# Meta tokens and inputs loaded in one transfer, the first unit of weights split tile by tile, squares behind the splits

## What is computed

```python
h = jnp.concatenate([meta, x], axis=1)
h = h + 0.5 * _swiglu(_rms_norm(h, norm_ffn1[l]), ffn1_w_gate[l], ffn1_w_up[l], ffn1_w_down[l])
def _rms_norm(x, g):
    y = xf * lax.rsqrt(jnp.mean(xf * xf, axis=-1, keepdims=True) + EPS)
    return (y * g.astype(jnp.float32)).astype(x.dtype)
def _swiglu(x, w_gate, w_up, w_down):
    return (jax.nn.silu(x @ w_gate) * (x @ w_up)) @ w_down
```

## Time and profile before

| | us |
|---|---|
| median of 3 runs | 2344.92 |
| lowest, highest | 2344.82, 2347.24 |
| profiled execution, its own time | 2350.06 |
| its span in the profile | 2348.3 |
| TensorE busy in the span | 2316.8 (99%) |
| VectorE, ScalarE, GpSimd busy | 1504.5, 1041.7, 194.3 |

### The profile page before, as it was taken

The page is one execution under the profiler, slowest core; times in us unless marked ns, Lnnn a source line. Parts: engine busy times, 40 slices in busy tenths (PEclk is TensorE's granted clock), DMA queues, the critical chain, the costliest instruction groups (busy, mean ns, idle before and its releaser), DMA issues.

```text
span 2348.3 us, 47351 instructions
## 1 busy us (share of the span) xinstructions
PE 2316.8 (99%) x17980; PEld 2211.4 (94%) x17980; DVE 1504.5 (64%) x2073; ACT 1041.7 (44%) x1277; POOL 194.3 (8%) x264
## 2 busy tenths in 40 slices
PE   8999999999999999999999999999999999999997
PEld 8999999999999999999999999998888888888886
DVE  6555544467554578888777666557666655666655
ACT  5343433445543343435555544445444433444443
POOL 0000010289200020002000000000000000000000
PEclk9999999999999999999999999999999999999998
DMA  7555555555555545555555545665665655656653
GB/s 214 175 173 175 172 178 175 174 172 171 182 172 174 167 137 170 162 168 160 155 160 159 163 136 180 197 186 174 195 185 182 193 185 185 188 179 196 186 187 119
DMA packets 416922, 408.66 MB, mean 174 GB/s; under 512 B 19408, under 2 KB 416720, under 8 KB 416848
## 3 DMA queue, kind: packets, MB, share of 16 engines
q1 hardware_dynamic: 411856, 407.03, 56.3%
q10 hardware_dynamic: 4992, 0.60, 0.2%
HBM read 405.48 MB, written 2.10 MB: 174 GB/s over the span
## 4 chain that ended last, share of the span: by engine, by line
PE 96%; DVE 2%; ACT 1%; issue 0%; DMA 0%; ACTq 0%; DVEq 0%; SPq 0%
PE ps L358 31%; PE ps L356 21%; PE ps L357 21%; PE ps L353 20%; PE ps L530 0%; PE ps L474 0%; DVE w_lo L902 0%; DVE xs L1058 0%; DMA raw<-gate 0%; ACT w_hi L599 0%; PE ps L523 0%; DVE scr L925 0%; ACT xs L621 0%; PE ps L537 0%; ACT scr L608 0%
## 5 line engine op out<-in xcount | busy, mean ns | idle before, releaser
L902 DVE TENSOR_TENSOR w_lo<-raw,w_hi 128x1024 fp32r<-128x1024 f32 x765 | 949.0, 1246 | 631.4 <-ACT w_hi L599 624.2
L358 PE MATMUL ps<-xs,w_lo 128*128 128x256 f32 (+2 forms) x4416 | 1260.0, 285 | 0.0
L599 ACT ACTIVATE w_hi<-raw 128x1024 fp32r<-128x1024 f32 x765 | 805.0, 1058 | 940.5 <-PE ps L358 931.6
L356 PE MATMUL ps<-xs,w_hi 128*128 128x272 f32 (+2 forms) x3008 | 866.7, 288 | 10.1 <-DVE xs L1058 3.5
L357 PE MATMUL ps<-xs,w_hi 128*128 128x272 f32 (+2 forms) x3008 | 863.9, 287 | 0.0
L358 PEld LDWEIGHTS ps<-xs,w_lo 128*128 128x128 f32 x4416 | 836.6, 189 | 0.0
L356 PEld LDWEIGHTS ps<-xs,w_hi 128*128 128x128 f32 x3008 | 570.3, 190 | 15.6 <-issue 10.1
L357 PEld LDWEIGHTS ps<-xs,w_hi 128*128 128x128 f32 x3008 | 572.8, 190 | 0.0
L353 PE MATMUL ps<-xs,w_hi 128*128 128x512 f32 x1408 | 493.3, 395 | 0.3 <-DVE w_lo L902 0.3
L358 PE MATMUL ps<-hs,w_lo 128*128 (+2 forms) x1408 | 402.6, 286 | 0.0
L353 PEld LDWEIGHTS ps<-xs,w_hi 128*128 128x128 f32 x1408 | 264.5, 188 | 61.2 <-issue 0.6
(11 more groups left out here) (249 smaller groups left out, 1602.0 us busy)
## 6 DMA issues: line engine op xcount, KB each, us to landing
raw<-gate SPq DMA_DIRECT2D x176, 512.0 KB, 4.5
raw<-up SPq DMA_DIRECT2D x176, 512.0 KB, 3.8
raw<-down SPq DMA_DIRECT2D x176, 512.0 KB, 4.3
raw<-w_in SPq DMA_DIRECT2D x168, 512.0 KB, 3.5
raw<-w_out SPq DMA_DIRECT2D x32, 512.0 KB, 4.2
raw<-w_proj SPq DMA_DIRECT2D x24, 512.0 KB, 4.7
raw<-glu_a SPq DMA_DIRECT2D x8, 512.0 KB, 3.4
raw<-glu_b SPq DMA_DIRECT2D x8, 512.0 KB, 3.4
```

The costliest lines, as they stand in the source:

```text
L356: pe.matmul(out, hi, xh, start=start and k == 0, stop=False)
L358: last = pe.matmul(out, lo, xh, start=False, stop=stop and k == KT - 1)
L599: act.activation(w_hi[:, slot, :, :], raw[:, slot, :, :], ACT.Copy).then_inc(hi_ready, 1)
L902: tt(w_lo[:, slot, :, :], raw[:, slot, :, :], w_hi[:, slot, :, :].bitcast(f32), SUB).then_inc(lo_ready, 1)
```

## The change

- **One transfer for `h`.** The host puts meta tokens and inputs into one array `hT` (rows of 272 floats). `metaT` and its wait are gone.
- **Unit 0 tile by tile.** SyncE loads tile 0 of `h`, tile 0 of the weights, tile 1 of both, then tiles 2 and 3 of both, then whole units. ScalarE and VectorE scale and split unit 0 tile by tile, and TensorE waits per tile (`first_lo`); in units 0 to 3 it goes by tiles of `x` (`by_tile`).
- **Splits first.** For units 1 to 3 the split of the weights comes ahead of the scalings. The squares come behind the split of unit 4; the splits of units 5 and of 6 to 8 are put among and behind them. Squares 0 to 2 are computed by GpSimd.
- **Norm later.** `norm(0)` is issued behind unit 5 instead of unit 3.
- **Small transfers** go from ScalarE to SyncE, between the loads of units 8 to 11, and the small operations on `lb` to the end of the first half of the network.
- **Start.** GpSimd sets `ones` first; `keep_warm` needs only that and makes 9 products instead of 14.

```diff
-                sp.wait_ge(lo_ready, u + 1)
+                if not isinstance(u, int) or u >= RING:
+                    sp.wait_ge(lo_ready, u + 1)
...
-            def load_x(c):
-                sp.dma_start(h[:, 4 * c:4 * c + 4, META:T],
-                             xT.rearrange("(k p) t -> p k t", p=P)[:, 4 * c:4 * c + 4, :]).then_inc(x_in[c], 16)
-                if c == 0:
-                    sp.dma_start(h[:, :, 0:META], metaT.rearrange("(k p) t -> p k t", p=P)).then_inc(meta_in, 16)
+            def load_x(k0, k1, landed):
+                sp.dma_start(h[:, k0:k1, :], hT.rearrange("(k p) t -> p k t", p=P)[:, k0:k1, :]).then_inc(landed, 16)
+            def load_first(w):
+                for c, (k0, k1) in enumerate(((0, 1), (1, 2), (2, 4))):
+                    load_x(k0, k1, x_first[c] if c < 2 else x_in[0])
+                    sp.dma_start(raw[:, 0, k0:k1, :], w.rearrange("(k p) n -> p k n", p=P)[:, k0:k1, 0:NC])\
+                        .then_inc(w_first[c] if c < 2 else raw_ready[0], 16)
+                for j in range(1, 4):
+                    load_x(4 * j, 4 * j + 4, x_in[j])
+                    load(j, w, j, 0, j)
+            def load_small(j):
+                if j == 0:
+                    sp.dma_start(sv[:, 0:3, :], s5v).then_inc(small_in[1], 16)
+                    sp.dma_start(lb[:, :, :], hg_lb).then_inc(small_in[2], 16)
+                elif j == 1:
+                    sp.dma_start(hgn[:, :], hg_norm).then_inc(small_in[3], 16)
+                    sp.dma_start(dsk[:, :], s5d).then_inc(small_in[4], 16)
+                elif j == 2:
+                    sp.dma_start(btmp[:, 0:2 * ST * GP].rearrange("p (r j c) -> p r j c", r=2, j=ST), s5b)\
+                        .then_inc(small_in[5], 16)
+                else:
+                    sp.wait_ge(consts, 2)
+                    for g in range(2):
+                        sp.dma_start(cd[64 * g:64 * g + 64, :, :, g * GP:(g + 1) * GP], s5c[64 * g:64 * g + 64])\
+                            .then_inc(small_in[6 + g], 16)
             def ffn(w_gate, w_up, w_down, q):
                 first = 0
                 for blocks in HALVES:
...
                     if peeled:
-                        column_block(w_gate, 0, 0, load_x)
+                        load_first(w_gate)
                         column_block(w_up, 0, 1)
-                    with sp.Fori(peeled, blocks) as b:
+                        column_block(w_gate, NC, 2, load_small)
+                        column_block(w_up, NC, 3)
+                    with sp.Fori(2 * peeled, blocks) as b:
                         column_block(w_gate, (b + first) * NC, b * 2 + q)
                         column_block(w_up, (b + first) * NC, b * 2 + q + 1)
                     q += 2 * blocks
@@ -339,13 +370,18 @@
...
+                first = isinstance(u, int) and u < RING
+                if not first:
+                    pe.wait_ge(lo_ready, u + RING + 1)
                 by_column = [(c, k) for c in range(2) for k in range(KT)]
                 by_row = [(c, k) for k in range(KT) for c in range(2)]
                 for c, k in by_column if need is None else by_row:
                     if need is not None and c == 0:
                         pe.wait_ge(x_ready, need + k + 1)
+                    if first and c == 0 and j == 0 and k < KT - 1:
+                        pe.wait_ge(first_lo, k + 1)
+                    elif first and c == 0 and k == (0 if j else KT - 1):
+                        pe.wait_ge(lo_ready, u + RING + 1)
...
                 for _ in range(n):
-                    pe.matmul(ps[:, bank, 0:P], ones[:, :], ident[:, :], start=True, stop=True)
+                    pe.matmul(ps[:, bank, 0:P], ones[:, :], ones[:, :], start=True, stop=True)
...
             def column_block(q, banks, c0, x_need, between=None, fresh=False, wide=False):
                 for j in range(4):
-                    if j or not fresh:
+                    by_tile = fresh and (j == 0 or isinstance(q, int) and q == 0)
+                    if not by_tile:
                         pe.wait_ge(x_ready, x_need + 4 * j + 4)
                     unit(j, 4 * q + j, banks, T - c0, rows(xs, 4 * j, c0, T - c0), j == 0, j == 3,
-                         None if j or not fresh else x_need, wide)
+                         x_need + 4 * j if by_tile else None, wide)
...
                         column_block(b * 2 + q, 0, c0, f * 2 * DT, fresh=mean, wide=f == 1)
-                        if mean:
+                        if mean and f:
                             norm(2 * f, c0)
                         pe.wait_ge(hidden, b + done + 1)
-                        column_block(b * 2 + q + 1, 2, c0, f * 2 * DT, wide=f == 1)
+                        column_block(b * 2 + q + 1, 2, c0, f * 2 * DT,
+                                     lambda j: norm(0, c0) if mean and not f and j == 1 else None, wide=f == 1)
...
-            pe.wait_ge(consts, 2)
-            keep_warm(14, 0)
+            pe.wait_ge(ones_ready, 1)
+            keep_warm(9, 0)
+            pe.wait_ge(consts, 1)
...
                     def block(b, mean=False):
-                        for j in range(1 if mean and not f else 0, 4):
+                        start = mean and not f
+                        for j in range(3 if start else 0, 4):
                             split(b * 2 + q, j)
+                        if start:
+                            split(b * 2 + q + 1, 0)
+                            split(b * 2 + q + 1, 1)
                         if mean:
                             root(2 * f, c0)
-                        split(b * 2 + q + 1, 0)
+                        if not start:
+                            split(b * 2 + q + 1, 0)
...
-                        for j in range(1, 4):
+                        for j in range(2 if start else 1, 4):
...
             act.wait_ge(small_in[0], 16)
-            for c in range(4):
+            for k in range(KT):
+                act.wait_ge(x_first[k] if k < 2 else x_in[0], 16)
+                upper(0, 0, k)
+                act.wait_ge(w_first[k] if k < 2 else raw_ready[0], 16)
+                act.activation(w_hi[:, 0, k, :], raw[:, 0, k, :], ACT.Copy).then_inc(first_hi if k < KT - 1 else hi_ready, 1)
+            for c in range(1, 4):
+                act.wait_ge(raw_ready[c], 16)
+                act.activation(w_hi[:, c, :, :], raw[:, c, :, :], ACT.Copy).then_inc(hi_ready, 1)
                 act.wait_ge(x_in[c], 16)
                 for k in range(4 * c, 4 * c + 4):
                     upper(0, 0, k)
-                if c < LEAD:
-                    act.wait_ge(raw_ready[c], 16)
-                    act.activation(w_hi[:, c, :, :], raw[:, c, :, :], ACT.Copy).then_inc(hi_ready, 1)
-                else:
-                    split(0, 0)
-                if c < 2:
-                    square(0, 0, 2 * c)
-                    square(0, 0, 2 * c + 1)
-            act.dma_start(sv[:, 0:3, :], s5v).then_inc(small_in[1], 16)
-            act.dma_start(lb[:, :, :], hg_lb).then_inc(small_in[2], 16)
-            act.dma_start(hgn[:, :], hg_norm).then_inc(small_in[3], 16)
-            act.dma_start(dsk[:, :], s5d).then_inc(small_in[4], 16)
-            act.dma_start(btmp[:, 0:2 * ST * GP].rearrange("p (r j c) -> p r j c", r=2, j=ST), s5b).then_inc(small_in[5], 16)
-            for k in range(4, DT // 2):
+            split(0, 1)
+            act.wait_ge(sq_ready, 3)
+            for k in range(3, DT // 2):
                 square(0, 0, k)
-            for g in range(2):
-                act.dma_start(cd[64 * g:64 * g + 64, :, :, g * GP:(g + 1) * GP], s5c[64 * g:64 * g + 64])\
-                    .then_inc(small_in[6 + g], 16)
+                if k == 4:
+                    split(0, 2)
...
                         else:
                             tt(gate, ps[:, 0:2, 0:T], inverse, MUL).then_inc(gated, 1)
-                        split(b * 2 + q + 1, 0)
+                        if not start:
+                            split(b * 2 + q + 1, 0)
                         dve.wait_ge(sig_ready, b + done + 1)
                         tt(gate, gate, sig, MUL).then_inc(silu, 1)
-                        split(b * 2 + q + 1, 1)
+                        if not start:
+                            split(b * 2 + q + 1, 1)
                         dve.wait_ge(silu, b * 2 + 2 * done + 1)
                         tt(gate, gate, inverse, MUL).then_inc(silu, 1)
...
+                    if between and not first:
+                        between(0)
...
+                if stage == 0:
+                    dve.wait_ge(small_in[2], 16)
+                    step(tt(lbt[:, 2, :], lb[:, 0, :], lb[:, 1, :], ALU.max))
+                    step.join()
+                    step(tt(lbt[:, 0, :], lb[:, 0, :], lbt[:, 2, :], SUB))
+                    step(tt(lbt[:, 1, :], lb[:, 1, :], lbt[:, 2, :], SUB))
...
             dve.wait_ge(small_in[0], 16)
-            for c in range(4):
+            for k in range(KT):
+                lower(0, 0, k)
```

(37 more changed lines are left out.)

22 lines of the change are left out of this document (9 added, 13 removed).

## The result

| | before | after |
|---|---|---|
| median of 20 runs | 2345.43 us | 2342.19 us |
| lowest and highest | 2343.23, 2347.65 | 2340.69, 2343.89 |
| profiled execution | 2350.06 | 2342.97 |
| its span, its mean granted clock | 2348.3, 0.993 | 2341.3, 0.995 |

The ratio is 0.9987, with a 95% interval of 0.9981 to 0.9993. The kernel is 3.2 us (0.13%) faster, where 7.2 were forecast: a real gain, but inside the 0.2% that the prediction called no change, and 0.8 us above the upper end of its range. The two profiled executions are 7.1 us apart, as summed.

The account below looks back on a forecast made before the run. TensorE's own matmuls (96% of the span) were taken as the bound. Terms up to the ninth unit, 1.45+1.2+2.87+2.8-0.8-0.3 = 7.2 us, gave 2344.9-7.2 = 2337.7 us, range 2334.8 to 2341.4.

Parts of the forecast that it names:

- gap ahead of unit 2: Start of the kernel: squares no longer stand between units 2 and 3, so the wait goes, 1.2 us won.
- wait ahead of unit 4: Cd transfers leave ScalarE's queue and the norm moves behind unit 5, so TensorE's wait goes: 2.87 us won.
- unit 5 waits for the squares' chain: Squares and additions now stand among the splits, so unit 5 is ready late: 0.8 us lost.
- unit 6 starts: ScalarE's split of unit 6 stands behind the last square: 0.3 us lost, start at 31.5.
- load of unit 11: Queued behind the cd pair, issued at some 39.3, landing near 43; 1.4 us of cover remain, costs nothing.
- rival C: GpSimd's third square meets unit 1's lower split, which starts 1.2 us later: 2338.9, chance 0.08.
- the term of 2.8 us for the half clock: TensorE's clock is at half from 30 to 36 us in before; with the gap gone, 2.8 us won.
- loads' term: Without the meta transfer, loads land 1.4 us earlier; unit 1 starts at 13.25 instead of 14.70, 1.45 us won.
- A: Clock falls after TensorE's 2.05 us idle behind unit 0, costing 1.7 us net: 2339.4, chance 0.25.
- B: Start of the kernel: nothing lands earlier from memory, unit 1 at 14.65, first term gone: 2339.1, chance 0.10.
- D: Weights land 1 us or more earlier still, VectorE's 2.97 per unit paces: 2336.7 to 2336.3, chance 0.12.
- E: Slower than before: the low clock holds on from unit 1, above 2345, chance 0.02.

Follow-up runs that it names:

- b_again: The kernel before, unchanged, measured once more: 2346.16 us, ratio 1.0002.
- a_again: The kernel after, unchanged, measured once more: 2342.27 us, ratio 0.9986.
- b_filled: Before, with 11 more products that nobody reads filling TensorE's wait ahead of unit 4: 2345.10 us, ratio 1.0.
- b_cd_moved: Before, with only the two cd transfers moved from ScalarE's queue to SyncE's, ahead of unit 11's load: 2342.88 us, ratio 0.9989.
- b_one_load_cd: Before, with one transfer for meta tokens and inputs and the cd pair moved to SyncE: 2340.74 us, ratio 0.9981.
- b_one_load: Before, with only the one transfer for meta tokens and inputs: 2342.90 us, ratio 0.9991.
- a_unit0_whole: After, with unit 0's input and weights in one transfer each, split, scaled and multiplied as a whole: 2341.74 us, ratio 0.9985.
- a_pad: After, with the rows of hT padded in memory from 1088 to 1280 bytes: 2342.24 us, ratio 0.9988.
- a_filled: After, with 16 warm-up products for 9 and 5 more between units 0 and 1: 2342.16 us, ratio 0.9988.
- a_all_filled: After, with fills at the start, in two waits of the projection behind the second norm and ahead of the last head: 2340.59 us, ratio 0.9982.
- b_two_filled: Before, with the one transfer, the cd pair on SyncE, and fills behind the second norm and ahead of the last head: 2339.81 us, ratio 0.9976.
- a_whole_filled: After, with unit 0 whole, 25 warm-up products instead of 9, and the three later waits filled: 2340.13 us, ratio 0.9981.

## Why the prediction was wrong

**The mechanism was right.** Held against the profile, the steps stand:

| step | forecast | in after's profile |
|---|---|---|
| unit 1's weights land, unit 1 starts | 10.4, 13.25 | 11.2, 13.98 |
| gap ahead of unit 2 | gone | gone (it starts at 17.1, was 18.94) |
| wait ahead of unit 4 | gone | gone (23.1, was 29.91 behind the norm) |
| unit 5 waits for the squares' chain | 0.8 | 0.51 |
| unit 6 starts | 31.5 | 32.00 |
| unit 8 starts | 37.55 | 38.10 |
| the span | 2341 | 2341.3 |

That the last row agrees is in part luck. After's profile has the clock low for 6.8 us at the last head, as before's has; with the 0 of b_again and a_again there, the two spans are 2343.0 and 2339.4.

The load of unit 11 is covered as said. SyncE's timeline in after:

```profile
32.31 3.29 SPq L314 DMA_DIRECT2D cd<-s5c  x2
35.64 2.51 SPq L269 DMA_DIRECT2D raw<-gate  x1
```

It is issued at 35.64, was forecast at 39.3, and landed at 41.4; TensorE waited nowhere there. GpSimd's squares and VectorE's lock are there too, in GpSimd's and VectorE's timeline:

```profile
6.00 2.34 POOL L1396 TENSOR_TENSOR scr<-h 128x544 f32<-128x544 f32 x2 [2.39 <-DMA h<-hT]
...
6.43 0.95 DVE L952 SCALAR_TENSOR_TENSOR xs<-h,gain,xs 128x272 fp32r<-128x272 f32 x1 [1.57 <-ACT xs L660]
7.31 1.31 DVE L1086 TENSOR_TENSOR w_lo<-raw,w_hi 128x256 fp32r<-128x256 f32 x1
```

A lower half took 0.95 us for the 0.50 of the first one, a quarter's split 1.31 for the first one's 0.42. It cost nothing, since unit 1's weights were not there yet; rival C did not come. The Trainium skill (SBUF — State Buffer, Who interferes with whom) gives VectorE and GpSimd one shared, exclusively locked port pair; the trace agrees, as it did at the earlier trace rows.

**The step that failed is the term of 2.8 us for the half clock**, with the sentence that carried it over to the median: "the saving is in absolute microseconds, so 2344.9-7.2". The 7.2 were the distance to one execution of before, and that execution was not like the median. It held 6.8 us of low clock in each of three places (30, 828, 1364) besides some 11 at its end, and took 5.1 us more than the median shown. The prediction had that 5.1 in its hands, and added the 2.8 of the first low stretch to the saving all the same. b_filled shows what that term is worth in the median: 0, with 2.1 as the end of its interval. Two more pairs agree: b_cd_moved gains 2.3 where 2.3 to 2.9 us of wait went, and b_one_load_cd is 2.2 ahead of b_one_load where 2.5 went. None of them rules out a microsecond. Without it, and with the typical wait of 2.3 (b_again; 2.2 between b_filled and b_cd_moved) for the 2.87, the prediction's own sum is 1.45+1.2+2.3-0.8-0.3 = 3.9: 2341.0. The other two parts of the distance to 2342.2 are the loads (0.7, below) and the median of before, which is 2345.4 over 20 runs and was 2344.9 over the three shown (0.5).

All 108 executions of before that ran beside the experiments bear this out. Sorted by their mean granted clock:

| mean clock | 0.993 | 0.994 | 0.995 | 0.996 | 0.997 | 0.998 |
|---|---|---|---|---|---|---|
| executions | 1 | 1 | 21 | 31 | 39 | 15 |
| mean time, us | 2350.0 | 2348.5 | 2346.7 | 2345.4 | 2344.5 | 2343.4 |

The profile shown of before, 2350.06 at 0.993, is not among them and is like the one at their slow end. After's 20 go the same way (0.995: 2343.2, 0.996: 2342.2, 0.997: 2341.1), 3.2 to 3.5 us below before at the same clock, between the 3.9 and the 3 that a_again was to tell apart. So most of a kernel's spread goes with its low-clock time. Each column of this table is another start from which a saving would have been counted.

**The loads' term** was mis-sized, in the part that is left: 1.45 us forecast, 0.72 seen. The prediction took 1.4 us of traffic from the missing transfer of `meta` and did not ask what the six small transfers in its place do. a_unit0_whole and b_one_load show it: from 3 to 8 us the same bytes in whole transfers pass at 367 and 360 GB/s, in small ones at 256. Before 3 us the small ones are ahead (from 2 to 3 us after moves 270 GB/s, a_unit0_whole 112), so the first eight microseconds are the fair stretch; in before, after and b_one_load:

```profile
0.00:8.00 8.00, 4.34 (x20) 4.34 (x21) 2.14 (x5) 3.24 (x6) 2.76 (x13) 1.00 0.70 166
```

```profile
0.00:8.00 8.00, 4.94 (x24) 4.75 (x24) 3.26 (x5) 4.03 (x9) 4.77 (x15) 1.00 0.69 196
```

```profile
0.00:8.00 8.00, 4.34 (x23) 4.34 (x24) 2.61 (x6) 4.23 (x8) 2.76 (x13) 1.00 0.78 237
```

After has moved 8x(196-166) = 240 KB more than before, 0.7 us of traffic at the prediction's 356 GB/s: the 0.72 seen. b_one_load has moved 568 KB more, 1.6 us: what ScalarE's queue gained there. The missing transfer alone is worth 1.7 us in the median.

**What adds up.** Take each profile's start of unit 8, less what low clock in front of it cost (3.4 us of it cost 1.5, by b_again against b_filled), and compare with 41.2, before's without it (b_filled):

| kernel | unit 8 | without low clock | ahead of 41.2 | gain in the median |
|---|---|---|---|---|
| b_cd_moved | 38.95 | 38.95 | 2.2 | 2.3 |
| b_one_load | 41.54 | 40.0 | 1.2 | 1.7 |
| b_one_load_cd | 37.19 | 37.19 | 4.0 | 3.9 |
| after | 38.10 | 38.10 | 3.1 | 3.2 |
| a_pad | 37.78 | 37.78 | 3.4 | 2.8 |
| a_filled | 37.96 | 37.96 | 3.2 | 2.9 |
| a_unit0_whole | 38.22 | not taken out | 3.0 | 3.3 |
| a_all_filled | 38.20 | 38.20 | 3.0 | 4.4 |
| b_two_filled | 37.02 | 37.02 | 4.2 | 5.5 |
| a_whole_filled | 36.62 | 36.62 | 4.6 | 4.5 |

Where only the start differs, the place by which the prediction counted gives the time within 0.6 us. a_all_filled and b_two_filled, with fills at the later waits, have 1.4 and 1.3 us on top. a_whole_filled has these fills too and seems to lack the gain; by the median spans, which leave out what lies around them, it is 5.5 us ahead, 0.9 on top.

**The rivals.** A was real but small: in the profile of after the clock fell during unit 0 (9 to 12 us), where it cost nothing, and in a_again behind unit 0, for one microsecond where the prediction had 1.7. B was half true, for another reason than the one it named. C, D and E did not come.

**What a low stretch costs depends on what waits behind it.** At the second norm it costs nothing. The same three places in the timeline of before and then of b_again are the first unit behind that norm, the next unit that waits for `u`, and, behind the last head, the one that waits for `qfv`:

```profile
822.74 0.36 PE L356 MATMUL ps<-xs,w_hi 128*128 128x272 f32 x1 [0.87 <-DVE xs L1058]
...
853.41 0.38 PE L356 MATMUL ps<-xs,w_hi 128*128 128x256 f32 x1 [0.71 <-ACT u L755]
...
1383.35 0.36 PE L356 MATMUL ps<-zs,w_hi 128*128 128x256 f32 x1 [0.70 <-ACT qfv L755]
```

```profile
820.63 0.36 PE L356 MATMUL ps<-xs,w_hi 128*128 128x272 f32 x1 [0.86 <-DVE xs L1058]
...
851.31 0.39 PE L356 MATMUL ps<-xs,w_hi 128*128 128x256 f32 x1 [0.71 <-ACT u L755]
...
1378.24 0.36 PE L356 MATMUL ps<-zs,w_hi 128*128 128x256 f32 x1 [0.70 <-ACT qfv L755]
```

Before has the clock low for 6.8 us in each part, b_again in neither; the first part takes 30.67 and 30.68 us, the second 529.94 and 526.93. All 14 profiles agree:

| low clock in the part | second norm, to `u` | last head, `u` to `qfv` |
|---|---|---|
| none | 30.67 to 30.71 (7 profiles) | 526.9 to 527.3 (7) |
| 3.4 us | 30.68 to 30.73 (6) | 528.3 to 528.8 (5) |
| 6.8 us | 30.67 (before) | 529.9 (before, after) |

At the second norm a unit at full clock waits 1.62 and 0.59 us for VectorE afterwards (after's timeline above); one at the low level, in before's, is followed by no such wait. Behind the last head nothing absorbs the loss: some 1.5 or 3.0 us. So the gain of the fills belongs to the last head's, and those at the second norm are worth nothing. This is also why the two spans are 7.0 apart and not near 10, though before's profile has one low stretch more behind unit 8.

**Open**: why six small transfers pass at 256 GB/s. Their issues take 0.41 to 0.47 us for 128 or 136 KB each, some 290 GB/s for the first four, so SyncE's issuing is a candidate, but the rate stays low to 8 us, and no run took the size alone apart. Open too is what decides whether the clock falls behind a given gap.

## What to carry to other kernels

Before a saving that hangs on TensorE's clock is added, look at the mean clock and the time of several executions: a profile 5 us above the median is itself the warning that it holds low stretches which the median has not. Count the saving from the same kernel without them, and take the clock as spread, not as a term. Then ask of each low stretch whether something behind it waits anyway: here the same stretch cost nothing at the second norm and its full loss at the last head.

The two cheap edits alone gave as much as the times can tell from the whole change: no long-running issue on a queue that feeds the bound engine, and no transfer of thousands of small pieces ahead of the first loads. A first unit that starts earlier gains nothing while the second waits for memory, and what it costs in small transfers is paid by everything behind it.

Where TensorE waits for other engines and nothing behind the wait absorbs a slow stretch, as ahead of the last head (2.48 us), products that nobody reads are worth having: they moved no unit and gained about 1.3 us in the median, and b_two_filled's runs spread over 0.8 us, where before's spread over 4.4 (a_all_filled's over 3.0, of which its spans show 1.6). Where the slow unit would have waited anyway, as at the second norm, they gain nothing.

## What the runs showed of the hardware

**The same gap, and two outcomes.** After a gap of 2.62 us the granted clock fell to 0.50 (1.2 GHz) in before's profile, after one of 2.63 it stayed at 1.00 (2.4 GHz) in after's; at unit 4 it fell behind 2.87, 2.51 and 2.30 us. Of the 11 profiles without fills at the later waits, 7 have it low behind the 2.6 us of the second norm and 7 behind the 2.5 of the last head, and they are not the same 7. Where it fell, it was back after 3.4 us or after 6.8 in every profile of this study, apart from the 8 to 12 us at the kernel's end. The Trainium skill (TensorE: Matmul & The Clock Gate, Why this matters for your kernels) warns of idle gaps between bursts of matmuls; the runs agree on the direction, but a gap of 2.6 us did both, so that in this kernel it can be reckoned with only as a chance.

**The clock column misses the start.** In after it reads 1.00 from 3 to 8 us, though the 18 warm-up instructions took 4.18 us, 0.23 each; twenty of them took 2.40 at a_all_filled's second norm, 0.12 each. For the first microseconds the durations tell the level, as the prediction read them.

**Small first transfers cost traffic.** The first four tiles of inputs and weights in six transfers of 128 to 272 KB, in place of two whole ones, took the microseconds from 3 to 8 from 367 to 256 GB/s; 2048 pieces of 64 bytes did about as much in before (249).

**A pair of transfers holds its queue.** The two `cd` transfers took 4.26 us on ScalarE's queue in before, 3.29 on SyncE's in after and 5.18 there in b_cd_moved; the same work, harmless where the queue has slack.
